# Head normalisation of a forgetting-attention kernel: squares by ScalarE, Newton step in PSUM, next row maximum inside it

## What is computed

```python
def _rmsnorm(x, g):
    inv = lax.rsqrt(jnp.mean(x * x, axis=-1, keepdims=True) + 1e-6)
    return x * inv * g

def _attn_layer(x, norm_g, w_in, b_f, q_g, k_g, w_out):
    proj = einsum('bsd,de->bse', _rmsnorm(x, norm_g), w_in)
    q, k, v, z, f_logit = split(proj)
    q, k = _rmsnorm(to_heads(q), q_g), _rmsnorm(to_heads(k), k_g)
    c = cumsum(log_sigmoid(f_logit + b_f), axis=-1)
    s = q @ k.T / sqrt(64) + c[:, None] - c[None, :]      # causal mask
    o = softmax(s) @ v
    return x + (o * silu(z)) @ w_out
```

## Time and profile before

| | |
|---|---|
| median of 3 runs | 1167.88 us (1167.59 to 1168.44) |
| the profiled execution, own time | 1168.07 us |
| its span, first to last instruction | 1166.3 us |
| busy PE / DVE / POOL / ACT | 1124.6 / 780.7 / 610.2 / 577.9 us |
| mean granted TensorE clock | 0.991 |
| one pair of heads in the loop | 77.8 us (PE busy 76.6, DVE 55.1, ACT 49.0, POOL 46.5) |

### The profile page before, as it was taken

The page is one execution under the profiler, slowest core; times in us unless marked ns, Lnnn a source line. Parts: engine busy times, 40 slices in busy tenths (PEclk is TensorE's granted clock), DMA queues, the critical chain, the costliest instruction groups (busy, mean ns, idle before and its releaser), DMA issues.

```text
span 1166.3 us, 16887 instructions
## 1 busy us (share of the span) xinstructions
PE 1124.6 (96%) x5640; PEld 918.3 (79%) x5640; DVE 780.7 (67%) x1062; ACT 577.9 (50%) x982; POOL 610.2 (52%) x400
## 2 busy tenths in 40 slices
PE   4999999999999998999999999999999999978998
PEld 3788888888888877787887878878878788767887
DVE  6997778666774247667677686776776867775541
ACT  5552323232344333655756757557567575575410
POOL 2236565465646425466575665665756656655410
PEclk8999999999999999999999999999999999989999
DMA  6202201211055211200110101001101010002142
GB/s 217 73 1 72 73 34 39 72 72 64 9 163 183 73 73 36 65 19 19 38 38 19 36 19 37 19 18 37 37 16 39 19 37 19 18 19 91 56 158 76
DMA packets 20255, 64.15 MB, mean 55 GB/s; under 512 B 2928, under 2 KB 3056, under 8 KB 20208
## 3 DMA queue, kind: packets, MB, share of 16 engines
q1 hardware_dynamic: 20064, 63.53, 16.2%
q10 hardware_dynamic: 144, 0.00, 0.0%
HBM read 54.88 MB, written 8.65 MB: 54 GB/s over the span
## 4 chain that ended last, share of the span: by engine, by line
PE 87%; DVE 7%; issue 3%; ACT 2%; POOL 1%; DMA 0%; ACTq 0%; DVEq 0%
PE ps L567 33%; PE ps L581 26%; PE ps L662 7%; PE ps L754 6%; PE ps L714 5%; PE ps L735 5%; DVE neg_max L1663 1%; DVE newton L1718 1%; PE ps L777 1%; PE ps L718 1%; PE ps L575 1%; PE ps L686 1%; DVE newton L1714 1%; DVE newton L1716 1%; PE ps L770 0%
## 5 line engine op out<-in xcount | busy, mean ns | idle before, releaser
L567 PE MATMUL ps<-h_hi,w_hi 128*128 128x512 f32 x632 | 267.3, 423 | 7.3 <-DVE h_lo L1809 2.5
L567 PE MATMUL ps<-h_hi,w_lo 128*128 128x512 f32 x632 | 249.2, 394 | 0.0
L567 PE MATMUL ps<-h_lo,w_hi 128*128 128x512 f32 x632 | 248.1, 393 | 0.0
L1874 POOL TENSOR_TENSOR a_lo<-raw,a_hi 128x512 fp32r<-128x512 f32 x94 | 139.3, 1495 | 152.6 <-ACT a_hi L951 152.4
L581 PE MATMUL ps<-b_hi,a_hi 128*128 128x512 f32 x456 | 179.6, 394 | 8.6 <-DVE b_lo L1372 8.5
L581 PE MATMUL ps<-b_lo,a_hi 128*128 128x512 f32 x456 | 178.3, 391 | 0.0
L581 PE MATMUL ps<-b_hi,a_lo 128*128 128x512 f32 x456 | 178.2, 391 | 0.0
L567 PEld LDWEIGHTS ps<-h_hi,w_lo 128*128 128x128 f32 x632 | 119.0, 188 | 27.2
L1913 POOL TENSOR_TENSOR w_lo<-w_raw,w_hi 128x1024 fp32r<-128x1024 f32 x39 | 99.2, 2544 | 78.3 <-ACT w_hi L923 78.1
L1922 POOL TENSOR_TENSOR p_big<-p_big,rdenom 128x896 f32<-128x896 f32 (+1 forms) x64 | 93.9, 1467 | 87.7 <-DVE rdenom L1671 87.6
L567 PEld LDWEIGHTS ps<-h_hi,w_hi 128*128 128x128 f32 x632 | 120.3, 190 | 23.5 <-issue 5.1
(11 more groups left out here) (182 smaller groups left out, 2107.1 us busy)
## 6 DMA issues: line engine op xcount, KB each, us to landing
w_raw<-in_w_ain SPq DMA_DIRECT2D x32, 512.0 KB, 3.4
raw<-in_w_cin SPq DMA_DIRECT2D x28, 512.0 KB, 4.3
xy<-in_x SPq DMA_DIRECT2D x16, 512.0 KB, 4.9
raw<-in_w_cout SPq DMA_DIRECT2D x8, 512.0 KB, 4.2
x_dram<-xy SPq DMA_DIRECT2D x8, 512.0 KB, 4.0
w_raw<-in_w_aout SPq DMA_DIRECT2D x8, 512.0 KB, 4.0
out<-y SPq DMA_DIRECT2D x7, 512.0 KB, 6.8
raw<-in_w_cin SPq DMA_DIRECT2D x8, 256.0 KB, 8.9
```

The costliest lines, as they stand in the source:

```text
L567: last = mm(ps[:, bank, :], st[slot][:, k, :], mov(k)[:, halves(h)], start=(at == 0 and (when or k == 0) and st is w_hi and mov is mov_hi) ...
L1874: TT(a_lo[:, i % RING, :, :], entry_source(i), a_hi[:, i % RING, :, :].bitcast(F32), ALU.subtract).then_inc(s_alo, 1)
```

## The change

- ACT makes both `sq_raw` (Square, float32) and `sq_hi` (a rounding copy of `sq_raw`). POOL's multiplication and its waits are gone, and POOL only subtracts.
- N2 and N3 write their result over the mean square in PSUM (`ms`, bank `B_MISC`), and N3 and N4 read it there. Only N1 still writes `newton`.
- In iterations 1 to 7, `row_max(i + 1, 0)` for i = 2 to 5 is issued between N2 and N3 of step i, and no longer at the start of step i + 1.

```diff
--- before.py
+++ after.py
@@ -283,7 +283,7 @@
         s_qkraw = sem("qk_evacuated")
         s_vz = sem("vz_evacuated")
         s_qsq = sem("qk_squared")
-        s_sqp = sem("squares_made_by_gpsimd")
+        s_sqp = sem("head_squares_made")
         s_sql = sem("squares_lo_made")
         s_ssq = sem("head_square_done")
         s_guess = sem("head_rsqrt_guessed")
@@ -1288,7 +1288,11 @@
 
                 if counted(4 * it + u):
                     act.wait_ge(s_ssq, 4 * it + u)
-                A(sq_hi[:, :], (qn, kn)[u // 2][:, halves(u % 2)], ACT.Square).then_inc(s_qsq, 1)
+                if u == 0 and counted(2 * it):
+                    act.wait_ge(s_vtr, 2 * it)
+                A(sq_raw[:, :], (qn, kn)[u // 2][:, halves(u % 2)], ACT.Square).then_inc(s_sqp, 1)
+                act.wait_ge(s_sqp, 4 * it + u + 1)
+                A(sq_hi[:, :], sq_raw[:, :], ACT.Copy).then_inc(s_qsq, 1)
 
             def z_silu(it):
 
@@ -1705,19 +1709,21 @@
 
             NEWTON = 3
 
-            def refine(it, u, base, local):
-
-                dst = (qn, kn)[u // 2][:, halves(u % 2)]
+            def refine(it, u, base, local, between=None):
+
+                dst, ms = (qn, kn)[u // 2][:, halves(u % 2)], ps[:, B_MISC, :]
                 dve.wait_ge(s_guess, 8 * it + 2 * u + 2)
                 if counted(2 * it):
                     dve.wait_ge(s_vtr, 2 * it)
                 TT(newton[:, :], y0[:, :], y0[:, :], ALU.mult).then_inc(s_dve, 1)
                 dve.wait_ge(s_dve, base + local + 1)
-                STT(newton[:, :], ps[:, B_MISC, :], EPS, newton[:, :], ALU.add, ALU.mult).then_inc(s_dve, 1)
+                STT(ms, ms, EPS, newton[:, :], ALU.add, ALU.mult).then_inc(s_dve, 1)
+                if between:
+                    row_max(it, between, 0)
                 dve.wait_ge(s_dve, base + local + 2)
-                STT(newton[:, :], newton[:, :], 3.0, y0[:, :], ALU.subtract, ALU.mult).then_inc(s_dve, 1)
+                STT(ms, ms, 3.0, y0[:, :], ALU.subtract, ALU.mult).then_inc(s_dve, 1)
                 dve.wait_ge(s_dve, base + local + 3)
-                STT(dst, dst, (gq, gk)[u // 2][:, :], newton[:, :], ALU.mult, ALU.mult).then_inc(s_qkn, 1)
+                STT(dst, dst, (gq, gk)[u // 2][:, :], ms, ALU.mult, ALU.mult).then_inc(s_qkn, 1)
                 return local + NEWTON
 
             def qk_evac(it, u):
@@ -1751,7 +1757,7 @@
                 for i in range(8):
                     own, at = (it, i - 1) if i else (it - 1, 7)
                     chunks = STEPS[at][1] + 1 if (att and i) or (before and not i) else 0
-                    if att:
+                    if att and not (proj and 3 <= i <= 6):
                         row_max(it, i, 0)
                     if att and i and STEPS[i - 1][1] in (1, 3) and (i >= 2 or before):
 
@@ -1788,7 +1794,7 @@
                     if att:
                         invert(it, i, 1)
                     if proj and 2 <= i <= 5:
-                        local = refine(it, i - 2, base, local)
+                        local = refine(it, i - 2, base, local, i + 1 if att else None)
                     if not att and i in (2, 4, 5):
                         forget((2, 4, 5).index(i))
                     if proj and i == 7:
@@ -1923,15 +1929,7 @@
 
             def square_lo(it, u):
 
-                src = (qn, kn)[u // 2][:, halves(u % 2)]
                 pool.wait_ge(s_qsq, 4 * it + u + 1)
-                if u == 0:
-                    if counted(2 * it):
-                        pool.wait_ge(s_vtr, 2 * it)
-                else:
-                    pool.wait_ge(s_ssq, 4 * it + u)
-                TT(sq_raw[:, :], src, src, ALU.mult).then_inc(s_sqp, 1)
-                pool.wait_ge(s_sqp, 4 * it + u + 1)
                 TT(sq_lo[:, :], sq_raw[:, :], sq_hi[:, :].bitcast(F32), ALU.subtract)\
                     .then_inc(s_sql, 1)
```

## The result

The changed kernel takes 1155.74 us (median of 5 runs, 1155.23 to 1155.96) against 1167.88 (5 runs, 1167.58 to 1169.57): a ratio of 0.9893 with a 95% interval of 0.9878 to 0.9907, or 12.1 us less. Forecast were 1154.3 and a range of 1151.0 to 1160.8; the measured time is 1.4 us above the forecast. Its profiled execution took 1155.84 us, with a span of 1154.0.

A forecast was written before the change was run, and what follows sets the result against it. PE, holding 87% of the chain, was taken to wait 1.87 us a pair at step 5's start. 11.6 - 0.7 + 2.7 = 13.6 us off 1168.07 gave 1154.5, forecast as 1154.3, range 1151.0 to 1160.8.

The forecast's parts named there:

- Place and number of the waits: PE's few waits all fall at the start of step 5, for `sq_lo`, `p_small` and `pt_lo`: 1.87 us a pair.
- N3 and N4 from 2.95 to 1.43 us in step 4: DVE's Newton step in step 4: with one input in PSUM, N3 takes 0.69 us and N4 0.74.
- The rule on PSUM as a source: N3 and N4 on DVE: 120 fixed cycles from PSUM against 58 from SBUF, 0.065 us each, left out of the sum.
- POOL's subtraction done by 692.5: Before step 5's square sum: subtraction starts at 690.86, takes 1.60 us at most; PE wants it at 693.26.
- ACT's copy covered: ACT in step 4: the added 0.62 us copy falls in idle time; uncovered, the exponential would slip 0.62 at most.
- Step 5, 1.65 us a pair: Start of step 5 on PE: 1.65 us of the 1.87 us of waiting goes, with `pt_lo` still late by 0.2.
- Step 3, 0.1 us a pair: First `pt_lo` of step 3 comes 0.4 to 0.5 us later; PE loses 0.1 us a pair, bounds 0 and 0.45.
- Step 4, taken as nothing: The maximum moved in step 3 makes step 4's exponential earlier; no credit was taken.
- The loop's sum: Seven pairs: 11.6 us less 0.7 for step 3; the pair's period goes from 77.8 to 76.2 us, 1.55 less.
- Pair 0, 2.7 us: Pair 0 has no maxima; shorter N4s and earlier squares save 2.7 us, bounds 1.8 and 3.5, with no clock fall.
- the limit on the next square sum: In pair 0 it waits for the chain forget gate, ACT, POOL, so only 1.8 us come through up to it.
- three waits, each ended by its own part: Step 5 on PE: 0.88 us at the square, 0.56 at the scores, the rest of 1.87 us at `pv`.

The follow-up runs named there:

- The last experiments: Two runs on S + N: N3 reading PSUM but writing SBUF, 1154.66 us; N3 reading two SBUF tensors and writing PSUM, 1161.76 us.
- the version with the late `out_gate`: S + N with only step 4's maximum moved, and `out_gate` of steps 3 and 5 issued behind the first two `pt_lo`: 1150.69 us.
- S alone: The kernel before with only the squares changed (ACT makes both, POOL only subtracts): 1171.52 us, ratio 1.0026.
- N alone: The kernel before with only the Newton step moved to PSUM: 1155.87 us, ratio 0.9885.
- S + N: The kernel before with squares on ACT and the Newton step in PSUM, no maximum moved: 1152.82 us, ratio 0.9862.
- M: The kernel before with only the four maxima moved, Newton step in SBUF and squares by POOL: 1190.08 us, ratio 1.0181.

## Why the prediction was right, point by point

- **Place and number of the waits.** Right for step 5, where PE's waits of the earlier trace rows are gone and 0.22 us for `pt_lo` is left (forecast: 0.2). But not all fell at that one place: 0.26 us a pair stood at the second scores of step 4.
- **N3 and N4 from 2.95 to 1.43 us in step 4.** Right: 0.69 + 0.75 = 1.44. The last experiments show the reason that the forecast only argued, the inputs. The output in PSUM costs N2 8 ns (699 against 691).
- **The rule on PSUM as a source.** The Trainium skill, "VectorE: DVE Perf Modes", section on the TRN2 errata, would, by the forecast's estimate from its figures, make N3 and N4 0.065 us longer than from SBUF. N3 takes 0.690 from PSUM, and 0.691 was its minimum from SBUF, so the measurement decides against that difference here.
- **POOL's subtraction done by 692.5, 0.7 us before it is wanted.** Right, with 1.17 us of room: the subtraction took 1.28 and not 1.60.
- **ACT's copy covered.** Right for step 5: ACT still sat idle 0.51 us before the exponential.
- **Step 5, 1.65 us a pair.** Right: from the last projection matmul to the first `pv` it was 3.35 us (693.03 to 696.38) and is now 1.65 (688.78 to 690.43), so 1.70 less. The same starts take 1.43 us without any wait, in the version with the late `out_gate`, and not the 1.48 of the forecast.
- **Step 3, 0.1 us a pair.** This term was mis-sized, and by its own numbers. The forecast had `pt_lo` 0.4 to 0.5 later (measured 5.60 - 5.15 = 0.45) and PE asking 0.2 after it was ready, and still took 0.1. The difference of the two, 0.2 to 0.3, was the value to take; measured 0.29 at the `pv`, and 0.34 from square sum to square sum. It also hoped for a faster `out_gate`. It was 0.68 instead of 0.92, but it waits 0.17 first.
- **Step 4, taken as nothing.** The forecast said of the moved maximum of step 3 that the exponential of step 4 comes earlier, and took no credit for it. It was worth 0.26 us a pair. The maximum did not have to move for it: the same three starts take 1.16 or 1.17 us in S alone, N alone and S + N too.
- **The loop's sum.** 1.70 + 0.26 - 0.34 = 1.62 us a pair, measured 1.60, forecast 1.55. That the period came out within 0.05 us is in part luck: the two mis-sized terms, 0.24 too little lost in step 3 and 0.26 not credited in step 4, cancel.
- **Pair 0, 2.7 us.** Right: 63.16 - 60.34 = 2.82, the clock did not fall, and the limit on the next square sum (it waits 1.13 us) was where the forecast had it.
- **The remaining 1.4 us.** The loop gave 7 x 1.60 = 11.2 us (forecast 10.9) and pair 0 gave 2.8 (2.7), together 14.0, but between the two profiled executions lie 1168.07 - 1155.84 = 12.2. The other 1.8 were lost before attention begins: the first square sum comes at 448.95 us, and at 447.13 in the kernel before, behind first-layer code that the change leaves alone. Up to 76 us the changed kernel is only 0.36 us behind; the granted clock over 14 to 30 us was 0.79 before and 0.68 after. Most of the rest arises near 105 us, where DVE waits for a weight load. Before, and then after:

```profile
105.26 0.69 DVE L1410 TENSOR_TENSOR s_t<-raw 128x512 f32<-128x512 f32 x1 [5.40 <-DMA raw<-in_w_cin]
```

```profile
107.43 0.69 DVE L1414 TENSOR_TENSOR s_t<-raw 128x512 f32<-128x512 f32 x1 [7.21 <-DMA raw<-in_w_cin]
```

The load is there 2.17 us later, PE then waits for `a_lo` (0.6 us of idle entry, none before), and by 147 us the kernel is 1.5 us behind. Why the load came later is not known. In the twelve traces of this study the first square sum comes at 446.6 to 447.7 us in four and at 448.3 to 449.3 in eight; the four have a granted clock of 0.79 over 14 to 30 us, the eight 0.68. Whether this belongs to a kernel or varies between executions was not tried.

What the forecast did not ask is which part does it. Its story was three waits, each ended by its own part. N alone gives nearly all of it: it takes the wait at the square from 0.88 to 0.11 us, because POOL's two instructions get shorter with it (0.44 us for `pt_lo` stays), and the early exponential comes just as well from a maximum left in place behind a shorter N3 and N4. S alone gives nothing in the loop, and on top of N it gives 0.22 us a pair (76.25 to 76.03). M was read as half of the cure and is a net cost. With all four maxima moved the period is 76.20 us, with none 76.03, with that of step 4 alone, the one step where the scores are complete when N2 ends, 75.89.

## What to carry to other kernels

A DVE instruction with two SBUF tensor inputs on a path where POOL is busy should be priced at the rest of POOL's running instruction plus most of its own length (0.55 of 0.69 us here), and one input in PSUM takes that away on both engines. Before moving an instruction forward in an in-order queue, compare its operand's ready time with the queue's time in every place that it moves to, and look at what it stood between: it may have hidden the wait of its neighbour. Where several engines' waits end within a microsecond of each other, shortening one only renames the wait, and the new one can be long enough to cost clock.

## What the runs showed of the hardware

- DVE held by POOL had no fixed price, but a fixed end. N3 alone was 0.69 to 1.54 us before, up to 2.24 with the maxima moved. In the kernel before, each of the 44 N3 and N4 that took over 0.8 us ended 0.54 to 0.56 us after the POOL instruction that was running when it started. The Trainium skill, "GPSIMD Engine Reference", section on specifications, names contention with DVE instructions with two SBUF inputs; these traces agree, and show it in both directions (POOL's multiplication is 1.04 us everywhere when N3 and N4 are off SBUF, 1.48 in the earlier trace rows).
- N1, which reads the same SBUF tensor twice, was never above 693 ns in either of the two kernels. It never started with more than 0.10 us of a running POOL instruction left, so that is no proof that it is exempt.
- The clock is not a function of one wait's length. After 1.49 us of waiting it fell to the lower level in three of seven pairs of S alone and stayed in the other four; in pair 0 it fell after 2.42 us and not after 1.6 or 1.7.
